# The first norm of a hybrid decoder block: how the squares are summed, the order of the low-rank and weight splits, and the place of one product

## The reference

```
h = x * rsqrt(mean(x*x, -1) + 1e-6) * g               # first norm
proj = h @ w_in                                       # conv | r,k,v | low-rank w,a,g | gates
# RWKV-7 branch, per step:
sa    = state @ (-kk_t)
state = state * w_t + sa (kk_t*a_t) + v_t k_t ;  y_t = state @ r_t
# then: x += (sig(gA)*conv + sig(gB)*rwkv) @ w_out ;  x += PEER(rmsnorm(x)) ;  final rmsnorm
```

## Time and profile before

| | |
|---|---|
| runs | 1708.61, 1708.95, 1709.91 us |
| profiled execution | 1708.64 us, its span 1706.8 us |
| TensorE busy | 1694.1 us (99%) |
| VectorE busy | 1393.3 us (82%) |
| ScalarE busy | 742.8 us (44%) |
| GpSimd busy | 675.9 us (40%) |

### The profile page before, as it was taken

One profiled execution on the slowest core, in us unless ns is written; L12 is line 12 of the kernel. 1 busy time (PEld: TensorE's weight loads), 2 busy tenths in 40 slices (PEclk: granted clock), 3 DMA queues, 4 the chain that ended last, 5 costly groups with the idle time before them and its releaser, 6 DMA issues.

```text
span 1706.8 us, 33761 instructions
## 1 busy us (share of the span) xinstructions
PE 1694.1 (99%) x12005; PEld 1498.7 (88%) x12005; DVE 1393.3 (82%) x2763; ACT 742.8 (44%) x1059; POOL 675.9 (40%) x555
## 2 busy tenths in 40 slices
PE   9999999999999999999999999999999999999998
PEld 6878888788888999999998888888888888888887
DVE  5379989565788999999996988887778888777886
ACT  5555445543423333477773433333333333333333
POOL 0000000010253666688873554443435444344440
PEclk9999999999999999999999999999999999999999
DMA  5221132253321555566669999999999999999982
GB/s 186 86 75 40 55 96 77 83 204 123 112 84 70 175 175 170 188 240 231 242 228 358 391 394 392 325 335 345 342 374 343 342 333 338 336 352 354 352 310 98
DMA packets 158288, 399.07 MB, mean 234 GB/s; under 512 B 12512, under 2 KB 78176, under 8 KB 156416
## 3 DMA queue, kind: packets, MB, share of 16 engines
q1 hardware_dynamic: 118496, 252.20, 42.2%
q0 software_dynamic: 39712, 145.77, 22.8%
HBM read 353.75 MB, written 44.04 MB: 233 GB/s over the span
## 4 chain that ended last, share of the span: by engine, by line
PE 84%; DVE 11%; DMA 2%; ACT 1%; issue 1%; SPq 1%; DVEq 0%; ACTq 0%
PE unit L425 84%; DVE oneh L2124 1%; DMA vraw<-v_tab 1%; DVE oneh L2114 1%; DVE ci L2100 1%; DVE ci L2095 1%; DVE oneh L2118 1%; DVE best L2098 1%; DVE cscr L2096 1%; DVE best L2093 1%; DVE cand L2089 1%; DMA g_dram<-ge 0%; SPq L1083 0%; DMA xin<-xT 0%; DVE accs L2201 0%
## 5 line engine op out<-in xcount | busy, mean ns | idle before, releaser
L425 PE MATMUL unit<-h2H,uH 128*128 128x384 f32 x1024 | 349.1, 341 | 0.2 <-ACTq L1493 0.2
L425 PE MATMUL unit<-h2L,uH 128*128 128x384 f32 x1024 | 343.8, 336 | 0.0
L2327 POOL DMA_INDIRECT ring<-u_tab,idx x128 | 204.1, 1594 | 221.1 <-DVE accs L2201 194.8
L425 PE MATMUL unit<-vH,aH 128*128 128x512 f32 x768 | 237.9, 391 | 0.7 <-DVE aL L2176 0.5
L425 PE MATMUL unit<-vH,aL 128*128 128x512 f32 x768 | 237.3, 390 | 0.0
L425 PE MATMUL unit<-vL,aH 128*128 128x512 f32 x768 | 237.2, 390 | 0.0
L2327 POOL DMA_INDIRECT ring<-v_tab,idx x128 | 149.8, 1171 | 198.5 <-DVE ring L2187 188.5
L425 PE MATMUL unit<-h2H,uL 128*128 128x384 f32 x1024 | 204.0, 336 | 0.0
L1167 ACT ACTIVATE ge<-unit 128x384 f32<-128x384 f32 x128 | 62.4, 487 | 321.2 <-PE unit L425 321.2
L425 PEld LDWEIGHTS unit<-h2H,uH 128*128 128x128 f32 x1024 | 192.5, 188 | 2.8 <-issue 0.4
L425 PEld LDWEIGHTS unit<-h2L,uH 128*128 128x128 f32 x1024 | 192.6, 188 | 2.4
(11 more groups left out here) (313 smaller groups left out, 3192.8 us busy)
## 6 DMA issues: line engine op xcount, KB each, us to landing
uraw<-uT SPq DMA_DIRECT2D x128, 512.0 KB, 7.3
vraw<-v_tab SPq DMA_DIRECT2D x128, 512.0 KB, 8.6
wraw<-wall SPq DMA_DIRECT2D x68, 512.0 KB, 3.7
w_dram<-wst SPq DMA_DIRECT2D x12, 2048.0 KB, 6.7
wg<-w_dram SPq DMA_DIRECT2D x31, 768.0 KB, 9.5
g_dram<-ge SPq DMA_DIRECT2D x64, 192.0 KB, 1.9
gl<-g_dram SPq DMA_DIRECT2D x32, 384.0 KB, 10.9
gate_dram<-gst POOLq DMA_DIRECT2D x16, 256.0 KB, 2.3
```

The source lines that it names most:

```text
L425: return pe.matmul(out, lhsT, rhs, start=start, stop=stop, skip_group_check=True)
L2327: pool.indirect_dma_start(out=ring[k][:, :], out_offset=None, in_=(u_tab, v_tab)[half], in_offset=bass.IndirectOffsetOnAxis(ap=idx[:, SR * ...
```

## The change

Five edits. (1) The squares are added by twos in place (`sq[c] += sq[c+1]`, four sums that don't depend on one another), and TensorE adds the four sums as well: it runs four groups of four one-column matmuls, each group after its sum, with one idle matmul of 256 columns between groups; its moving column is a tile of its own, `mean1`, set by VectorE. The idle matmuls ahead are six instead of nine. (2) ScalarE takes the root ahead of `wloH`. (3) `wloH` and `wloL` are made in two halves. (4) The first two `wH` are made in halves of 512 columns behind `hH` of chunks 2 to 5. (5) In `features_b` the product of `r_in` stands ahead of `ke` and `be`, and `token_major` waits for a semaphore of its own, `ends_ready`, before it reads them.

```diff
@@ tensor
             pe.wait_ge(idle_ready, 1)
-            idle(9, T)
-            pe.wait_ge(s_first, 32)
+            idle(6, T)
             o = begin("ms1", 0)
-            pe.wait_ge(sum_grown, DC)
-            for t in range(TT):
-                last = mm(o[:, t:t + 1], rs[:, tile(t)], C(C_M1024)[:, 0:1], t == 0, t == TT - 1)
+            pe.wait_ge(mean1_ready, 1)
+            for c in range(0, DC, 2):
+                pe.wait_ge(sum_grown, c + 2)
+                for t in range(TT):
+                    last = mm(o[:, t:t + 1], sq[:, c, tile(t)], mean1[:, :], c == 0 and t == 0, c == DC - 2 and t == TT - 1)
+                if c < DC - 2:
+                    idle(1, 256)
             last.then_inc(fill_sem("ms1"), 1)
             idle(1, 256)
+            pe.wait_ge(s_first, 32)
             pe.wait_ge(inverse4, 1)
...
-            pe.wait_ge(wlol_ready, 1)
             for c in range(DC):
+                if c % (DC // 2) == 0:
+                    pe.wait_ge(wlol_ready, 1 + c // (DC // 2))
                 pe.wait_ge(h_high, c + 1)
...
                 for parts in ((("nktT", nkt), ("vT", v_in[:, :, tile(t)])), (("beT", be), ("keT", ke))):
+                    if parts[0][0] == "beT":
+                        pe.wait_ge(ends_ready, t + 1)
@@ scalar
+            act.wait_ge(s_first, 32)
+            wait_filled(act, "ms1")
+            fn(root4[:, :], ps("ms1")[:, 0:TT], ACT.Sqrt, bias=vc("eps", 0)).then_inc(take_sem("ms1"), 1)
             act.wait_ge(s_lora, 16)
-            fn(wloH[:, :, :], wlo[:, :, :], ACT.Copy).then_inc(wloh_ready, 1)
-            wait_filled(act, "ms1")
-            act.wait_ge(s_first, 32)
-            fn(root4[:, :], ps("ms1")[:, 0:TT], ACT.Sqrt, bias=vc("eps", 0)).then_inc(take_sem("ms1"), 1)
-            split_h(0)
-            split_h(1)
+            for k in range(2):
+                some = slice(k * DC // 2, (k + 1) * DC // 2)
+                fn(wloH[:, some, :], wlo[:, some, :], ACT.Copy).then_inc(wloh_ready, 1)
             for c in range(DC):
                 act.wait_ge(h_new, c + 1)
                 fn(hH[:, c, :], h[:, c, :], ACT.Copy).then_inc(h_high, 1)
+                if 2 <= c < 6:
+                    n, some = c // 2 - 1, slice(c % 2 * DC // 2, (c % 2 + 1) * DC // 2)
+                    if c % 2 == 0:
+                        act.wait_ge(w_loaded[n], 16)
+                    ins = fn(wH[:, n, some, :], wraw[:, n, some, :], ACT.Copy)
+                    if c % 2:
+                        ins.then_inc(wh_ready, 1)
@@ vector
+            dve.memset(mean1[:, :], 1.0 / D).then_inc(mean1_ready, 1)
             dve.memset(zeros[:, :], 0.0).then_inc(idle_ready, 1)
...
-            tt(rs[:, :], sq[:, 0, :], sq[:, 1, :], ALU.add).then_inc(sum_grown, 2)
-            for c in range(2, DC):
-                dve.wait_ge(sq_ready, c + 1)
-                dve.wait_ge(sum_grown, c)
-                tt(rs[:, :], rs[:, :], sq[:, c, :], ALU.add).then_inc(sum_grown, 1)
+            for c in range(0, DC, 2):
+                if c:
+                    dve.wait_ge(sq_ready, c + 2)
+                tt(sq[:, c, :], sq[:, c, :], sq[:, c + 1, :], ALU.add).then_inc(sum_grown, 2)
...
+                dve.wait_ge(rk_ready, t + 1)
+                tt(r_in[:, :, tile(t)], r_in[:, :, tile(t)], ep[:, :, :], ALU.mult).then_inc(feats_ready, 1)
                 tick(tt(chunks(ke), chunks(kh), ends, ALU.mult))
                 after(b_)
-                tick(tt(chunks(be), chunks(bh), ends, ALU.mult))
-                dve.wait_ge(rk_ready, t + 1)
-                tt(r_in[:, :, tile(t)], r_in[:, :, tile(t)], ep[:, :, :], ALU.mult).then_inc(feats_ready, 1)
+                tt(chunks(be), chunks(bh), ends, ALU.mult).then_inc(ends_ready, 1)
@@ gpsimd
-            pool.wait_ge(wloh_ready, 1)
-            pool.tensor_tensor(wloL[:, :, :], wlo[:, :, :], wloH[:, :, :], ALU.subtract).then_inc(wlol_ready, 1)
+            for k in range(2):
+                some = slice(k * DC // 2, (k + 1) * DC // 2)
+                pool.wait_ge(wloh_ready, k + 1)
+                pool.tensor_tensor(wloL[:, some, :], wlo[:, some, :], wloH[:, some, :], ALU.subtract
+                                   ).then_inc(wlol_ready, 1)
```

More of the change, by code:

```diff
@@ L178, in build @@
     mm_ = at("mm_", 165, [P, 2, T])
+    mean1 = at("mean1", 11, [P, 1])
     h2H = at("h2H", 93, [P, DC, T], F32R)
@@ L324, in build @@
         xg_high, xg_split = sem("xg_high"), sem("xg_split")
-        zero_ready, idle_ready = sem("zero_ready"), sem("idle_ready")
+        zero_ready, idle_ready, mean1_ready = sem("zero_ready"), sem("idle_ready"), sem("mean1_ready")
+        ends_ready = sem("ends_ready")
         lerp_part, lora_part, lora_ready = (sem(n) for n in [
```

## The result

The changed kernel took 1715.59 us (median of 12 runs, 1709.95 to 1716.76), the kernel before, beside it on the same chip, 1709.79 (12 runs, 1708.12 to 1711.06): 1.0031 times as long, 95% interval 1.0024 to 1.0038. That is 5.3 us slower by the ratio. The forecast was 1708.3 and the upper end of its range 1710.2. The profiled execution took 1715.43, its span 1713.6, so 6.8 us more than the span of before (1706.8) have to be found. A kernel's runs scatter by some 3 us, which is why the profiles, and not the times alone, carry what follows.

A forecast was written before the change was run, and what follows sets the result against it. TensorE was taken to bound the kernel (84% of the chain), running without a break from 13.93 us for 93 us. Norm +0.6 and receptance -1.15 sum to -0.55, giving 1708.3 us, range 1706.3 to 1710.2.

The forecast's parts named there:

- The queue on TensorE: Opening norm: group plus idle matmul take 1.32 us, so the fourth group starts at 12.46, long after its sum.
- Rival 1: Opening norm: TensorE keeps up with the sums and the norm gains; total -2.2 us, 1706.4 to 1706.8; chance 0.10.
- the 25 ns: Floor for a matmul of 1 to 64 columns; by it a group costs 0.2 us and the norm gains 1.04.
- The norm at +0.6: Opening norm: TensorE's row of sums ends at 13.35 us instead of 12.70; loss of 0.6, ends 0.4 and 0.9.
- 0.43 either way: Opening: TensorE's slow start, hidden before, now stands on the path; one slow pass more or less is 0.43 us.
- Passes of 0.86 behind 5 us: Sign of a wrong forecast: TensorE passes of 0.86 us in the opening, later than 5 us.
- Rival 3: Opening: TensorE's clock falls during one-column groups and short zeros, costing 1.7 to 4.3 us; 1709.8 to 1712.7; chance 0.07.
- A new wait of half a microsecond between 123 and 240: Sign of a wrong forecast: a new wait of that length on TensorE, after the receptance product's place.
- Receptance at -1.15: `features_b(1)`: `r_in` ahead of `ke` and `be` removes TensorE's stall at 122.68 us, gaining 1.15, at least 0.99.
- Rival 2: Behind `features_b(1)`: the `r_in` gain is lost at the next join, leaving +0.6 us; 1709.2 to 1709.6; chance 0.15.
- Root, low-rank and weight splits at nothing: Opening and chunk loop: moving the root first and halving the splits costs or gains nothing, as TensorE's work covers it.

The follow-up runs named there:

- The tree: Changed kernel with VectorE adding squares in a tree, so TensorE has two one-column groups instead of four: 1710.46 us, 1.0004 of the kernel before.
- longer zeros: Changed kernel with idle matmuls of 512 columns instead of 256 between the groups: 1713.26 us, 1.0019 of the kernel before.
- the sums alone: Kernel before with only the sums by twos, the four groups on TensorE and six idle matmuls: 1715.33 us, 1.0032 of the kernel before.
- the padding of twelve: Changed kernel with the old sums, three of nine 512-column idle matmuls cut into fifteen of 102, twelve matmuls more: 1711.40 us, 1.0006 of the kernel before.
- receptance alone: Kernel before with only the `r_in` product ahead of `ke` and `be`, and `ends_ready`: 1709.49 us, 0.9996 of the kernel before.
- without the sums: Changed kernel with the sums as before, keeping edits 2 to 5: 1708.26 us, 0.9992 of the kernel before; run again 1708.61 us, 0.9996.
- 64 paddings: Changed kernel with the old sums and 64 short zero matmuls put ahead of the first norm: 1736.03 us, one run.
- nine more: Changed kernel without the three idle matmuls between the groups: 1711.63 us, 1.0013 of the kernel before.
- 32 or 64 more: Changed kernel with the old sums and 32 or 64 short zero matmuls ahead of the first norm: 1721.47 us with 32, 1736.03 with 64.
- the orders alone: Kernel before with only the root ahead of the low-rank split and the splits in halves: 1710.15 us, 1.0004 of the kernel before.

## Why the prediction was wrong

*The queue on TensorE: right.* No group waited for VectorE, the period was 1.32, and the sums were ready at 10.25 (forecast 10.5) without use. Rival 1 is out, and with it, as the price of this list, the 25 ns of the Trainium skill, "TensorE: Matmul & The Clock Gate", section "Back-to-back issue gap", which gives them as the gap of a matmul by itself, without its weight load. The tree's 0.111 us a pass, with nothing between, agrees with that page's section on LDWEIGHTS, 107 ns for 128 columns.

*The norm at +0.6: the term that failed.* It was +3.2. The plain queue makes 12.46 - 11.68 = 0.8 of it. The start of the zeros makes 1.1: twelve passes were costed at the length of the 18 of before less six fast ones, 8.5, but the slow ones went on longer. Their weight loads show as 0.34, the last at 4.18 us before and here, in the timeline of weight loads, at 6.77:

```profile
6.77 0.34 PEld L428 LDWEIGHTS unit<-zeros 128*128 128x128 f32 x1 [0.52 <-issue]
```

The prediction said itself that this length was hidden before and now stands on the path, "0.43 either way"; it was worth 1.1 in the profile. It also called the slow passes the lower clock level, by their pace of 0.86. The windows view shows a granted clock of 1.00 over that stretch in every profile, so why they are slow isn't shown by any run. "Passes of 0.86 behind 5 us" was one of its signs of being wrong, and it came true. The rest, 19.17 - 13.56 = 5.61 instead of 15.94 - 11.68 = 4.26, is 1.35 for the clock; where longer zeros kept it up it is 4.31.

*Rival 3, the clock falls in the opening: it came about, and had 0.07.* Its mechanism fits the profile, and longer zeros took it away. Its size, 1.7 to 4.3, holds the 3.0 of the sums alone (by the same working, 0.43 ahead of the fourth group and 19.90 - 13.04 - 4.26 = 2.60 behind it) but not the changed kernel's 1.35. The evidence against it was one group behind 0.61 idle in the trace of before, and that is no test of four groups in a row. Its 1709.8 to 1712.7 still falls short of the measurement.

*What no term and no rival held:* the standstills of TensorE between 123 and 400 us. "A new wait of half a microsecond between 123 and 240" was named as what would refute the forecast, and one of 1.31 stood there, but not for the reason in mind, a join: the twelve matmuls of the opening move all that follows in the program. The standstills make +1.4 in the profile; the padding of twelve made the one of 172 us without the new sums. That TensorE waits there for its own program is the likeliest reading (the packet a microsecond before, no releaser, a place that moves with the count of instructions) but isn't shown. A trace of before had its own, 0.4 us ended by `issue`, which I passed over when I read the waits ended by a named instruction only.

*Receptance at -1.15: right*, at 1.05; the first 64 x 64 matmul follows the last `wH` one by 0.32, not by the 0.23 of the forecast. Rival 2 is out: from the transposes of `nkt` in `token_major(0)` to those in `token_major(1)` it is 18.1 us before, and 17.0 in the changed kernel, with receptance alone, and without the sums. *Root, low-rank and weight splits at nothing: right* (1.0004 for them alone).

*The sum.* With the opening at +3.2, receptance -1.05 and the standstills +1.4, a run without a second fall would be +3.6; the profiled one had 1.7 of the second fall and 1.5 that I can't assign. The median (+5.3 to 5.8) lies between.

*Open:* why the clock falls near 335 us. It did in the profiles of the changed kernel, of the one with longer zeros, and at 356 with 64 paddings, and in none of the other ten. All three falls start at the same point of the program, about 1 us after the start of a group of eight 8-column matmuls, which ends 6.9 us of one-column matmuls (`csq`, a pair behind each matmul of 512 columns). Timeline of TensorE in the changed kernel:

```profile
333.66 0.28 PE L428 MATMUL unit<-cst,csq 128*128 128x1 f32 x2
333.80 1.04 PE L428 MATMUL unit<-sel,gsq 128*128 128x8 f32 x8
334.69 1.85 PE L428 MATMUL unit<-v_in,cst 128*128 128x512 f32 x2
```

So here too the clock falls behind matmuls that stream few columns. But the same stretch passes at the full clock in the other ten (`v_in` takes 1.10 or 1.11), no run changed it, and what decides isn't shown. Why TensorE stands still for long only at some places, though packets on the instruction queue come all along (54 in the span), isn't shown either. One run of the changed kernel had a mean clock of 1.000 and took 1709.95, less than the account allows, so the standstills too must differ between executions; the wide spread of the kernel with twelve more (5.6 us against 2.7 and 3.5 without) says the same.

## What to carry to other kernels

Moving sums to TensorE as one-column float32 matmuls costs a full weight load for each pass, 0.11 us, and behind such groups the clock fell, on the path; compare the engine's queue, not only the chain that is shortened. A wait behind the first work hides how slowly that work starts: when the wait goes, price the start at the worst profile, not at one. And instructions added at the start of a long unrolled program can bring a standstill of more than a microsecond far behind them, so a change of a few tenths of a microsecond should be tested against a padding of the same number of instructions.

## What the runs showed of the hardware

- TensorE stood still for 1.31 (changed kernel) and 1.45 us (twelve more) amid 32 like 64 x 64 matmuls, released by nothing in the trace, about 1 us after a 16 KB packet on the instruction queue. Twelve matmuls more at the start of the program brought it, nine more brought one of 1.08 us six passes further on; 32 or 64 more did not. That the list outruns its own program is the likely reading, not a shown one.
- Four groups of one-column matmuls with 256-column zeros between let the granted clock fall to its lower level for 3.4 us (changed kernel; 0.50 from 14.08 to 17.48) and 6.8 us (sums alone); with 512-column zeros it stayed at 1.00 in the opening of the profiled run, and the mean clock of the other ten was 0.999 or 1.000. Without zeros between, 32 passes in a row, it fell as well, amid the last passes, and the runs' mean clock was 0.997 to 0.999.
- How long the slow start of TensorE lasts differs between executions with like first instructions: the last slow weight load lies between 3.32 us (the orders alone) and 6.77 (the changed kernel) in the profiles, and twelve passes of zeros took 7.12 without zeros between the groups, 7.31 with the sums alone and 8.25 in the changed kernel. The granted clock reads 1.00 there in all of them.
